# A quarter of the gathered second rows summed on TensorE instead of VectorE, with sixteen gelu slots and twelve first products ahead

## Chip, cores and metric

One core of one Trainium2 chip. The metric is device time in microseconds (us), of which the median of several runs is quoted. The kernel before takes 1690.52 us, median of three runs (1689.63 to 1690.55).

## What is computed

One DeepNorm layer over 512 tokens of width 1024. The first half (attention with forget gates, a convolution branch, gates, an output projection, a layer norm) is not touched. The second half is a product-key expert retrieval: for every token the 128 best of 16384 experts (8 heads of 16) are found, each with a gate.

```python
ue = jnp.take(u_tab, ei, axis=0)
a = jnp.einsum('thkd,td->thk', ue, xi)
wgt = (jax.nn.gelu(a.astype(jnp.float32)) * gi).astype(xi.dtype)
ve = jnp.take(v_tab, ei, axis=0)
return jnp.einsum('thk,thkd->td', wgt, ve)
```

The result is scaled by a gate row, added to the layer's input and layer-normalised. All is float32.

## The kernel before, in words

**Two ways to the retrieval.** For 384 tokens (three tiles of 128, `TD = 3`) the kernel is dense: the expert table is cut into 128 chunks of 128 experts, and each chunk has a *first product* (u-chunk times tokens, 24 matmuls of 128x384), a gelu on ScalarE, a multiplication by the gates, and a *second product* (two halves of the v-chunk, each 9 matmuls of 128x512, since every product is made of a high and a low part in three matmuls, `three`, lines 1725 to 1729). For the last 128 tokens, the *own* tile, it is sparse: GpSimd gathers for every slot j of 128 (`SLOTS`) one row of the table per token, 128 rows of 4 KB. VectorE turns a gathered u-row into a dot product (`dot`, line 1384), and later adds a gathered v-row times its weight into `acc[:, TD, :]` (`own_row`, line 1616). The gathers land in a ring of eight slots; gather j waits until the slot's last user is done (lines 675 and 714).

**Stages.** The first 80 chunks (`SPILL`) have only their first product, beside the search for the experts; their gelu goes to memory (`gelu_ahead`) and comes back later as `gback`. Then `FILL = 8` further first products are made ahead (chunks 80 to 87, until `PRE = 88`), while the last gates are written to memory (`gates_by_key`). SyncE then loads the gates back (`gring`, line 547), the first v-chunks (`vraw`, line 522) and the rest of the u-chunks.

**Groups.** After that come 16 groups of 8 chunks (`GR = 8`). Group g has a first half of eight steps k (in each, while there are any left, one first product and the first half of second product k) and a second half of eight steps (the other half of second product k). Groups 0 to 4 make the first products of chunks 88 to 127; groups 5 to 15 have only second products. In each step VectorE makes the low part of a v-chunk (`low_v`, line 1584), in the first half of groups 0 to 4 also that of a u-chunk (`low_u`, line 1379), and in the second half the gated gelu of the next group (`weigh`, line 1572, and `low_w`, line 1578, between which ScalarE makes the high part, line 944). The instructions stand in a hand-written order on each engine. v-chunks have four converted slots (`VR`), and their raw rows four, eight from group 6 on.

**Quotas.** The dots are spread by `DOT_F` over the FILL steps and by `DOT_G` over the first-half steps of groups 0 to 4 (24 a group). The own rows are spread by `ROWS_OF` and `rows_at` evenly over all 16 steps of groups 4 to 14: 6, then 13 in each of eight groups, then 12 and 6. `gelz` has eight slots; the gelu of chunk c in the groups waits for `weigh` of chunk c - 88 (line 897 onwards). At the start of group 12 (`ROW_GROUP`) SyncE loads the layer's input `xfin` and two broadcast rows (lines 593 to 596, together 3 MB), ahead of that group's v-chunks. In the last group `own_sum` (line 1633) finishes the own tile in steps 4 and 5.

A matmul of 32 columns into a quarter of a bank's partitions stands already in the kernel at `mod_rows` (line 1816); sixteen of them run one behind the other.

Of the kernel before, what the change touches and what calls it, by code (L numbers as in the profile page):

```python
# [13 lines left out]
P = 128  # L14
# [81 lines left out]
ROWS_OF = (6,) + (13,) * 8 + (12, 6)  # L96
assert sum(ROWS_OF) == SLOTS

# [4 lines left out]
FILL = 8  # L103
# [3 lines left out]
PS = 8  # L107
VR = 4
# [3 lines left out]
DOT_F = (0, 0, 0, 1, 1, 2, 2, 2)  # L112
DOT_G = (3, 3, 3, 3, 3, 3, 3, 3)
# [12 lines left out]
W_GROUP = BESIDE - 2  # L126
V_GROUP = W_GROUP + 1
ROW_GROUP = NG - 4
assert len(DOT_F) == FILL and len(DOT_G) == GR
assert sum(DOT_F) + sum(DOT_G) * V_GROUP == SLOTS  # L130
# [3 lines left out]
def build(nc, x, cb, ccol, w_modn, b_modc, w_modt, wblk, b_fc, conv_wc, conv_vec, keys_t, u_t, u_tab, v_tab, rows, out):  # L134
    with ExitStack() as ctx:
# [50 lines left out]
        gelz = sb("gelz", [P, PS, TN], F32, 88)  # L186
        x2s = sb("x2s", [P, D], F32, 100)
# [19 lines left out]

        gback = sb("gback", [P, 3, 2, TN], F32, 4)
        xfin = sb("xfin", [P, TT, D], F32, 32)
# [30 lines left out]
        idxN = small("idxN", [P, SLOTS], I32)  # L240
        own_g = small("own_g", [P, SLOTS], F32)
# [118 lines left out]
        own_w = sem("own_w")  # L360
        own_v = sem("own_v")
        u_in = [sem(f"u_in{i}") for i in range(RAW)]
# [37 lines left out]
        def v_row(i):  # L400
# [6 lines left out]
            return row, v_in[slot], 16 * (uses + 1), before  # L407

# [59 lines left out]
        def _(sp):  # L468
# [89 lines left out]
            load_u(PRE)  # L558
# [6 lines left out]
            for c in range(PRE + 1, PRE + RAW):  # L565
                load_u(c)
# [23 lines left out]
            for g in range(NG):  # L590
                if g == ROW_GROUP:
                    sp.wait_ge(x1_out, 16)
                    sp.dma_start(xfin[:, 0:TD, :], x1_dram[1:TT].rearrange("t p d -> p t d")).then_inc(x1_in, 16)
# [3 lines left out]
                first_half(g)  # L597
# [16 lines left out]
        def _(pool):  # L614
# [94 lines left out]
            for j in range(SLOTS):  # L709
                if j < RING:  # L710
                    pool.wait_ge(dot_r, SLOTS - RING + j + 1)
                else:
# [3 lines left out]
                    in_offset=bass.IndirectOffsetOnAxis(ap=idxN[:, j:j + 1], axis=0)).then_inc(ring_in[j % RING], 16)  # L716

# [7 lines left out]
        def _(act):  # L725
# [167 lines left out]
            def gelu(c):  # L893
                m = c // 4
                act.wait_ge(u_mm, c + 1)
                if c >= PRE:
                    act.wait_ge(w_mul, c - PRE + 1)
                elif c % 4 == 0 and m > 1:
                    act.wait_ge(gel_out[m % 2], 16 * (m // 2))
                nc.scalar.activation(gelz[:, c % PS, :], bank[c % 2][:, 0:TN], ACT.Gelu_apprx_tanh).then_inc(gel_r, 1)  # L900
# [69 lines left out]
            def group(g, last=False):  # L970
                for k in range(GR):
# [3 lines left out]
                    if k and c < CH:  # L975
# [6 lines left out]
                if PRE + GR * g < CH:  # L982
                    gelu(PRE + GR * g + GR - 1)
                if g == W_GROUP:
                    act.wait_ge(dot_r, SLOTS)
                    nc.scalar.activation(own_a[:], own_a[:], ACT.Gelu_apprx_tanh).then_inc(own_gel, 1)
# [22 lines left out]
        def _(dve):  # L1009
# [407 lines left out]
            def select(s):  # L1417
# [97 lines left out]
                if s in numbers:  # L1515
                    link(last)
                    last = nc.vector.tensor_copy(numbers[s][:].rearrange("p (h k) -> p h k", k=TOPK), sel[:, 0, :, :])
                last.then_inc(sel_r, 1)
                beside(15)

            def transposed(s):

                dve.wait_ge(selT_mm, s)
                nc.vector.tensor_copy(selT[:, 2, :], bank[2][:, P:2 * P])
# [34 lines left out]
            def weigh(g, k):  # L1559
# [3 lines left out]
                if g < BESIDE:  # L1563
                    dve.wait_ge(gel_r, c + 1)
                    src = gelz[:, c % PS, :]
# [39 lines left out]
            own_next = iter(range(SLOTS))  # L1605

            def own_row():

                j = next(own_next)
                dve.wait_ge(ring_in[j % RING], 16 * ((SLOTS + j) // RING + 1))  # L1610
                if j == 0:
                    dve.wait_ge(own_w, 1)
                    nc.vector.tensor_scalar(acc[:, TD, :], ring[:, 0, :], own_a[:, 0:1], None, ALU.mult).then_inc(own_v, 1)
                else:
                    dve.wait_ge(own_v, j)
# [511 lines left out]
```

## Time and profile before

| quantity | value |
|---|---|
| median of three runs | 1690.52 us |
| the profiled execution | 1690.79 us, span 1689.0 us |
| TensorE, VectorE, ScalarE, GpSimd busy | 1566.8, 1388.3, 687.6, 678.0 us |
| chain that ended last | TensorE 60%, VectorE 25%, issue 5%, DMA 5%, ScalarE 3% |
| moved by DMA | 422.22 MB, 250 GB/s over the span |

The busy time of TensorE counts matmuls that overlap, so its share says little of how far it is from its limit; what matters is where it sits idle and who ends that. A row of the timeline reads: start in us, duration in us, engine, line, operation, output and input, how many are merged, and in brackets how long the engine had been idle and who ended that. "vlo L1584" is the low part of a v-chunk. A row of a stretch reads: its length, then the busy time of TensorE, its weight loads, VectorE, ScalarE and GpSimd with their instructions, the granted TensorE clock as a share of 2.4 GHz, the busy share of the DMA engines and the GB/s moved.

### The profile page before, as it was taken

Reading aid. Unit: us, or ns where it says so; the run is one execution under the profiler, and the core shown is the slowest. Engines: PE = TensorE matmul, PEld = TensorE weight load, DVE = VectorE, ACT = ScalarE, POOL = GpSimd, SP = SyncE. Lnnn points to the kernel's source line nnn. Section 1 sums busy time; section 2 is a strip of 40 time slices with the busy share of each in tenths; the row PEclk is TensorE's granted clock in tenths of the full one; section 3 lists DMA queues with packets and bytes.
Section 4 is the critical chain, followed back from the end, with each engine's and each line's share of the span. In section 5 each row is a group of like instructions: output and inputs, shape, how many; then the busy total and the mean of one; then the engine's idle time right before and its main releaser. Section 6 shows DMA issues by size and latency. Waiting matters only on the chain.

```text
span 1689.0 us, 22167 instructions
## 1 busy us (share of the span) xinstructions
PE 1566.8 (93%) x7772; PEld 1361.4 (81%) x7772; DVE 1388.3 (82%) x2725; ACT 687.6 (41%) x1037; POOL 678.0 (40%) x450
## 2 busy tenths in 40 slices
PE   5999999994999999999998999999988999998986
PEld 3887777773899999999997998988967777776775
DVE  5489776888489799979966987977978888887888
ACT  4335565424334345545553343343333333333342
POOL 0210000002035778677763844746643443333301
PEclk9999999997999999999999999999999999999999
DMA  8323234462676657667789989989899999999962
GB/s 350 100 76 125 88 100 162 149 205 83 229 253 206 176 159 185 180 192 183 205 229 351 395 325 339 374 310 367 285 338 366 357 382 378 362 385 384 364 223 81
DMA packets 180894, 422.22 MB, mean 250 GB/s; under 512 B 33584, under 2 KB 66480, under 8 KB 180528
## 3 DMA queue, kind: packets, MB, share of 16 engines
q1 hardware_dynamic: 90688, 264.44, 43.8%
q0 software_dynamic: 57200, 139.58, 24.9%
q10 hardware_dynamic: 32896, 16.78, 3.6%
q8 instruction: 63, 1.03, 0.2%
q14 instruction: 47, 0.39, 0.1%
HBM read 375.55 MB, written 45.15 MB: 249 GB/s over the span
## 4 chain that ended last, share of the span: by engine, by line
PE 60%; DVE 25%; issue 5%; DMA 5%; ACT 3%; SPq 0%; DVEq 0%; POOL 0%; ACTq 0%; POOLq 0%
PE bank L1727 18%; PE bank L1728 18%; PE bank L1729 18%; DVE vlo L1584 2%; DVE el L1578 2%; DVE wf L1572 2%; DVE one L1544 2%; DMA gring<-gates_by_key 2%; DVE wlo L1379 2%; DVE one L1542 2%; ACT eh L944 2%; DVE one L1546 2%; DMA gates_by_key<-stage 1%; PE bank L1873 1%; PE bank L2008 1%
## 5 line engine op out<-in xcount | busy, mean ns | idle before, releaser
L1727 PE MATMUL bank<-act_hi,whi 128*128 128x384 f32 (+1 forms) x1352 | 482.2, 357 | 12.7 <-ACT gelz L900 4.5
L1729 PE MATMUL bank<-act_hi,wlo 128*128 128x384 f32 (+1 forms) x1352 | 473.1, 350 | 0.0
L1728 PE MATMUL bank<-act_lo,whi 128*128 128x384 f32 (+1 forms) x1352 | 473.0, 350 | 0.0
L1727 PE MATMUL bank<-vhi,eh 128*128 128x512 f32 x768 | 306.7, 399 | 46.3 <-DVE vlo L1584 46.3
L1728 PE MATMUL bank<-vlo,eh 128*128 128x512 f32 x768 | 302.7, 394 | 0.0
L1729 PE MATMUL bank<-vhi,el 128*128 128x512 f32 x768 | 302.5, 394 | 0.0
L1727 PEld LDWEIGHTS bank<-act_hi,whi 128*128 128x128 f32 x1352 | 256.1, 189 | 30.9 <-issue 7.9
L1728 PEld LDWEIGHTS bank<-act_lo,whi 128*128 128x128 f32 x1352 | 256.0, 189 | 13.9
L1729 PEld LDWEIGHTS bank<-act_hi,wlo 128*128 128x128 f32 x1352 | 255.5, 189 | 13.4
L691 POOL DMA_INDIRECT gates_by_key<-selW,selS x128 | 233.6, 1825 | 70.0 <-issue 47.5
L675 POOL DMA_INDIRECT ring<-in_u_tab_dram,idxN x128 | 200.5, 1567 | 149.5 <-DVE ring L1384 98.0
L714 POOL DMA_INDIRECT ring<-in_v_tab_dram,idxN x128 | 151.2, 1182 | 231.6 <-DVE acc L1616 221.6
L1727 PEld LDWEIGHTS bank<-vhi,eh 128*128 128x128 f32 x768 | 145.9, 190 | 89.7 <-DVE vlo L1584 60.7
L953 ACT ACTIVATE vhi<-vraw 128x512 fp32r<-128x512 f32 x256 | 155.8, 623 | 138.6 <-PE bank L1729 130.3
L1584 DVE TENSOR_TENSOR vlo<-vraw,vhi 128x512 fp32r<-128x512 f32 x256 | 176.3, 696 | 36.2 <-ACT vhi L953 33.7
L1379 DVE TENSOR_TENSOR wlo<-raw,whi 128x1024 fp32r<-128x1024 f32 x108 | 131.9, 1222 | 59.1 <-ACT whi L891 57.2
L1729 PEld LDWEIGHTS bank<-vhi,el 128*128 128x128 f32 x768 | 146.0, 190 | 31.4
L1728 PEld LDWEIGHTS bank<-vlo,eh 128*128 128x128 f32 x768 | 146.1, 190 | 29.0 <-issue 0.5
L900 ACT ACTIVATE gelz<-bank 128x384 f32<-128x384 f32 x128 | 63.3, 494 | 260.2 <-PE bank L1729 247.1
L1616 DVE SCALAR_TENSOR_TENSOR acc<-ring,own_a,acc 128x1024 f32<-128x1024 f32 x127 | 162.6, 1280 | 0.0
L944 ACT ACTIVATE eh<-wf 128x384 fp32r<-128x384 f32 x128 | 67.2, 525 | 231.9 <-DVE wf L1572 229.4
L1384 DVE SCALAR_TENSOR_TENSOR ring<-ring,x2s 128x1024 f32<-128x1024 f32 x128 | 150.7, 1221 | 7.9 <-DMA ring<-in_u_tab_dram,idxN 6.6
(237 smaller groups left out, 1978.4 us busy)
## 6 DMA issues: line engine op xcount, KB each, us to landing
raw<-in_u_t_dram SPq DMA_DIRECT2D x128, 512.0 KB
vraw<-in_v_tab_dram SPq DMA_DIRECT2D x256, 256.0 KB
raw<-in_wblk_dram SPq DMA_DIRECT2D x61, 512.0 KB, 4.2
gring<-gates_by_key SPq DMA_DIRECT2D x32, 768.0 KB
raw<-in_w_modt_dram SPq DMA_DIRECT2D x32, 512.0 KB, 3.4
gates_by_key<-stage ACTq DMA_DIRECT2D x8, 2048.0 KB
gelu_ahead<-gelz SPq DMA_DIRECT2D x20, 768.0 KB
gback<-gelu_ahead SPq DMA_DIRECT2D x40, 384.0 KB
```

The lines of the kernel that those rows point to most:

```text
L675: pool.indirect_dma_start(out=ring[:, j % RING, :], out_offset=None, in_=u_tab, in_offset=bass.IndirectOffsetOnAxis(ap=idxN[:, j:j + 1], a ...
L691: pool.indirect_dma_start(out=gates_flat, out_offset=bass.IndirectOffsetOnAxis(ap=selS[:, n:n + 1], axis=0), in_=selW[:, n:n + 1], in_offs ...
L714: pool.indirect_dma_start(out=ring[:, j % RING, :], out_offset=None, in_=v_tab, in_offset=bass.IndirectOffsetOnAxis(ap=idxN[:, j:j + 1], a ...
L944: nc.scalar.activation(eh[:, k, :], wf[:, k % 2, :], ACT.Copy).then_inc(w_hi, 1)
L953: nc.scalar.activation(hi_slot, row, ACT.Copy).then_inc(v_hi, 1)
L1379: nc.vector.tensor_tensor(wlo[:, c % SPL, :], raw[:, c % RAW, :], whi[:, c % SPL, :].bitcast(F32), ALU.subtract).then_inc(u_lo, 1)
L1384: nc.vector.scalar_tensor_tensor(out=ring[:, j % RING, :], in0=ring[:, j % RING, :], scalar=1.0, in1=x2s[:], op0=ALU.mult, op1=ALU.mult, a ...
L1584: nc.vector.tensor_tensor(lo_slot, v_row(2 * GR * g + n)[0], hi_slot.bitcast(F32), ALU.subtract).then_inc(v_lo, 1)
L1616: nc.vector.scalar_tensor_tensor(out=acc[:, TD, :], in0=ring[:, j % RING, :], scalar=own_a[:, j:j + 1], in1=acc[:, TD, :], op0=ALU.mult, o ...
L1727: mm(o, wh, mh, start=start, stop=False)
L1728: mm(o, wh, ml, start=False, stop=False)
L1729: return mm(o, wl, mh, start=False, stop=stop)
```

## The change

Of the 128 v-rows of each own token, 96 (`OWN`) are still summed by VectorE. The other 32 (`QSLOTS`) go to TensorE in eight *quads*. One gather brings the 32 rows of four tokens into the 128 partitions; a quad is four such gathers (`qring`, 2 MB) and eight matmuls of 32 columns by 512, with weights that are zero but for the token's own column (`wz`). They accumulate in banks 0 and 1, which `own_sum` adds. One quad is made in each of groups 5 to 12, after step 10 of the group. The indices and weights are laid out for this once (`shared_out`, `transposed`, `eye`, one transpose in FILL, one in group 4). The quad's gathers stand on the GpSimd queue among the own gathers. FILL is 12 (`PRE = 92`), so that group 4 has four first products and not eight; `gelz` has sixteen slots. `DOT_G` has 27 dots a group in groups 0 to 3 and 8 in group 4. The own rows are 3 in group 4 and 9 or 10 in each of groups 5 to 14, six of them in the first half's first six steps. `xfin` is loaded after the first half of group 13 and waits for the last quad.

```diff
-FILL = 8
+SHARED = 4
+QSLOTS = P // SHARED
+OWN = SLOTS - QSLOTS
+QUADS = P // (4 * SHARED)
+IN_STRIP = QUAD // SHARED
+FILL = 12
+GS = 16
-DOT_F = (0, 0, 0, 1, 1, 2, 2, 2)
-DOT_G = (3, 3, 3, 3, 3, 3, 3, 3)
+DOT_F = (0, 0, 0, 1, 1, 1, 1, 1, 1, 2, 2, 2)
+DOT_G = (4, 3, 3, 4, 3, 3, 4, 3)
+DOT_W = (2, 2, 2, 2, 0, 0, 0, 0)
+OWN_AT = [(0, 0, 0, 0, 0, 0, 0, 0, 0, 0, 1, 0, 1, 0, 1, 0)] + [(1, 1, 1, 1, 1, 1, 0, 0, 0, 1, 0, 1, 0, 1, n, 0) for n in
+                                                                (1, 0, 0, 1, 0, 0, 1, 0, 0, 0)]
+QUAD_STEP = GR + 2
-W_GROUP = BESIDE - 2
+W_GROUP = (CH - PRE) // GR
-ROW_GROUP = NG - 4
+ROW_GROUP = NG - 3
...
+    _rows = sum(sum(n) for n in OWN_AT[:_i]) + sum(OWN_AT[_i][:QUAD_STEP]) + RING if _i else RING // 2
+    QUAD_ROWS[_rows] = _i
...
-            for c in range(PRE):
+            for c in range(PRE - 1):
                 load_u(c)
...
             for g in range(NG):
+                first_half(g)
                 if g == ROW_GROUP:
                     sp.wait_ge(x1_out, 16)
+                    sp.wait_ge(quad_mm, QUADS)
...
+            def quad_rows(i):
+                if i == 0:
+                    pool.wait_ge(selT_sb, TT - 1)
+                    pool.wait_ge(u_lo, low_before(CH)[0])
+                else:
+                    pool.wait_ge(quad_mm, i)
+                for j in range(4):
+                    four = j * IN_STRIP + i
+                    pool.indirect_dma_start(
+                        out=qring[:, j, :], out_offset=None, in_=v_tab,
+                        in_offset=bass.IndirectOffsetOnAxis(ap=idxT[:, four:four + 1], axis=0)).then_inc(quad_in, 16)
...
+            for j in range(OWN):
+                if j in QUAD_ROWS:
+                    quad_rows(QUAD_ROWS[j])
+                own_gather(j)
...
-                if c >= PRE:
-                    act.wait_ge(w_mul, c - PRE + 1)
+                if c >= SPILL + GS:
+                    act.wait_ge(w_mul, c - SPILL - GS + 1)
...
-                dve.wait_ge(own_v, SLOTS)
+                dve.wait_ge(own_v, OWN)
+                link(nc.vector.tensor_tensor(acc[:, TD, cut], acc[:, TD, cut], bank[half][:, :], ALU.add))
...
+                    if g == W_GROUP and k == 4:
+                        dve.wait_ge(wT_mm, 1)
+                        link(shared_out(wT, bank[0]))
+                        for j in range(4):
+                            part = slice(j * IN_STRIP, (j + 1) * IN_STRIP)
+                            nc.vector.tensor_tensor(wz[:, part, :],
+                                                    wT[:, part].unsqueeze(2).broadcast_to([P, IN_STRIP, QUAD]),
+                                                    eye[:], ALU.mult).then_inc(wz_r, 1)
...
+            def quad(i):
+                if i == 0:
+                    pe.wait_ge(wz_r, 4)
+                    pe.wait_ge(g_row, 2)
+                pe.wait_ge(quad_in, 64 * (i + 1))
+                for half in range(2):
+                    for j in range(4):
+                        last = mm(bank[half][j * QUAD:(j + 1) * QUAD, :], wz[:, j * IN_STRIP + i, :],
+                                  qring[:, j, half * HALF:(half + 1) * HALF], start=i == 0, stop=i == QUADS - 1)
+                last.then_inc(quad_mm, 1)
...
+                        if GR + k == QUAD_STEP and 0 <= g - V_GROUP < QUADS:
+                            quad(g - V_GROUP)
```

## Rows read from the trace of the kernel before

**Rows 1.** The page's costliest groups: busy, mean ns, idle before, releaser.
```profile
L1727 PE MATMUL bank<-vhi,eh 128*128 128x512 f32 x768 | 306.7, 399 | 46.3 <-DVE vlo L1584 46.3
...
L1616 DVE SCALAR_TENSOR_TENSOR acc<-ring,own_a,acc 128x1024 f32<-128x1024 f32 x127 | 162.6, 1280 | 0.0
...
L1384 DVE SCALAR_TENSOR_TENSOR ring<-ring,x2s 128x1024 f32<-128x1024 f32 x128 | 150.7, 1221 | 7.9 <-DMA ring<-in_u_tab_dram,idxN 6.6
```

**Rows 2.** TensorE's timeline: its wait before step 3, groups 8, 9, 11, 12, 14.
```profile
1379.18 0.50 PE L1727 MATMUL bank<-vhi,eh 128*128 128x512 f32 x1 [2.05 <-DVE vlo L1584]
...
1417.02 0.50 PE L1727 MATMUL bank<-vhi,eh 128*128 128x512 f32 x1 [2.05 <-DVE vlo L1584]
...
1494.29 0.50 PE L1727 MATMUL bank<-vhi,eh 128*128 128x512 f32 x1 [2.05 <-DVE vlo L1584]
...
1538.69 0.51 PE L1727 MATMUL bank<-vhi,eh 128*128 128x512 f32 x1 [1.81 <-DVE vlo L1584]
...
1614.31 0.50 PE L1727 MATMUL bank<-vhi,eh 128*128 128x512 f32 x1 [2.07 <-DVE vlo L1584]
```

**Rows 3.** TensorE's timeline: two second-product triples, one behind the other.
```profile
1655.28 0.39 PE L1727 MATMUL bank<-vhi,eh 128*128 128x512 f32 x1
1655.96 0.39 PE L1727 MATMUL bank<-vhi,eh 128*128 128x512 f32 x1
```

**Rows 4.** VectorE's timeline, one step in the second half of group 9.
```profile
1443.28 1.28 DVE L1616 SCALAR_TENSOR_TENSOR acc<-ring,own_a,acc 128x1024 f32<-128x1024 f32 x1
1444.47 0.69 DVE L1584 TENSOR_TENSOR vlo<-vraw,vhi 128x512 fp32r<-128x512 f32 x1
1445.08 0.55 DVE L1572 TENSOR_TENSOR wf<-gback,gring 128x384 f32<-128x384 f32 x1
1446.22 0.56 DVE L1578 TENSOR_TENSOR el<-wf,eh 128x384 fp32r<-128x384 f32 x1 [0.59 <-ACT eh L944]
1446.69 1.28 DVE L1616 SCALAR_TENSOR_TENSOR acc<-ring,own_a,acc 128x1024 f32<-128x1024 f32 x1
```

**Rows 5.** DMA by stretch (1371 to 1409, 1500 to 1530, 1388 to 1403 us).
```profile
DMA packets 5067, 14.27 MB, mean 375 GB/s; under 512 B 563, under 2 KB 563, under 8 KB 5065
...
DMA packets 3769, 11.99 MB, mean 400 GB/s; under 512 B 390, under 2 KB 390, under 8 KB 3767
...
DMA packets 1993, 6.10 MB, mean 407 GB/s; under 512 B 217, under 2 KB 217, under 8 KB 1993
```

**Rows 6.** Line 900 in 1000 to 1066 us (first and last start), and busy times there.
```profile
L900 ACT ACTIVATE gelz<-bank x9: 472/492/493, 999.6 to 1066.1; 128x384 f32<-128x384 f32 x9
...
1000.00:1066.00 66.00, 66.00 (x336) 60.14 (x335) 56.04 (x90) 24.49 (x40) 38.58 (x25) 1.00 0.92 345
```

**Rows 7.** Timelines of ScalarE, SyncE and TensorE around the end of FILL.
```profile
896.50 0.49 ACT L900 ACTIVATE gelz<-bank 128x384 f32<-128x384 f32 x1 [2.72 <-PE bank L1729]
...
893.66 0.33 SPq L547 DMA_DIRECT2D gring<-gates_by_key  x1
...
909.30 0.41 PE L1727 MATMUL bank<-act_hi,whi 128*128 128x384 f32 x1 [4.51 <-ACT gelz L900]
...
927.41 0.69 PE L1727 MATMUL bank<-act_hi,whi 128*128 128x384 f32 x1 [3.75 <-DVE wlo L1379]
```

**Rows 8.** TensorE's timeline: its waits where group 5 begins.
```profile
1251.49 0.50 PE L1727 MATMUL bank<-vhi,eh 128*128 128x512 f32 x1 [0.75 <-DVE vlo L1584]
1254.90 0.50 PE L1727 MATMUL bank<-vhi,eh 128*128 128x512 f32 x1 [1.08 <-DVE vlo L1584]
...
1260.32 2.72 PE L1933 MATMUL bank<-dg,consts 128*128 128x512 f32 x4 [3.08 <-DVE dg L1243]
```

**Rows 9.** TensorE's timeline: the 32-column matmuls of `mod_rows`.
```profile
35.89 1.92 PE L1816 MATMUL bank<-modn,cwide 128*32 128x512 f32 x16
```

**Rows 10.** The last group: `own_sum` on VectorE, and TensorE's wait behind it.
```profile
1648.65 0.68 DVE L1633 TENSOR_TENSOR acc<-acc,rows 128x512 f32<-128x512 f32 x1
...
1662.34 0.50 PE L1727 MATMUL bank<-vhi,eh 128*128 128x512 f32 x1 [2.82 <-DVE vlo L1584]
```

More of the change, by code:

```diff
@@ L125 @@
 ZEROS = 16
-W_GROUP = BESIDE - 2
+W_GROUP = (CH - PRE) // GR
 V_GROUP = W_GROUP + 1
-ROW_GROUP = NG - 4
+ROW_GROUP = NG - 3
 assert len(DOT_F) == FILL and len(DOT_G) == GR
-assert sum(DOT_F) + sum(DOT_G) * V_GROUP == SLOTS
+assert sum(DOT_F) + sum(DOT_G) * W_GROUP + sum(DOT_W) == SLOTS
+assert sum(sum(n) for n in OWN_AT) == OWN and V_GROUP + QUADS <= ROW_GROUP
+QUAD_ROWS = {}
+for _i in range(QUADS):
+    _rows = sum(sum(n) for n in OWN_AT[:_i]) + sum(OWN_AT[_i][:QUAD_STEP]) + RING if _i else RING // 2
+    QUAD_ROWS[_rows] = _i
+assert len(QUAD_ROWS) == QUADS
 assert [sum(n) for n in LOWS] == [STEPS[0], STEPS[2]]
@@ L240, in build @@
         idxN = small("idxN", [P, SLOTS], I32)
+        idxT = small("idxT", [P, QSLOTS], I32)
         own_g = small("own_g", [P, SLOTS], F32)
@@ L564, in _ @@
                 load_v(0, k, 0)
-            for c in range(PRE + 1, PRE + RAW):
+            for c in range(PRE - 1, PRE + RAW):
                 load_u(c)
@@ L1603, in last_sum @@
                 return bn(xfin, t, half)
[L1605 to L1615, printed above, removed]
-                    nc.vector.scalar_tensor_tensor(out=acc[:, TD, :], in0=ring[:, j % RING, :],
-                                                   scalar=own_a[:, j:j + 1], in1=acc[:, TD, :],
-                                                   op0=ALU.mult, op1=ALU.add).then_inc(own_v, 1)
@@ L1620, in rows_at, with own_rows @@
[L1620 to L1627 removed]
+            own_next = iter(range(OWN))
+            def own_rows(g, step):
+                at = g - W_GROUP
+                for _ in range(OWN_AT[at][step] if 0 <= at < len(OWN_AT) else 0):
+                    j = next(own_next)
+                    dve.wait_ge(ring_in[j % RING], 16 * ((SLOTS + j) // RING + 1))
+                    if j == 0:
+                        dve.wait_ge(own_w, 1)
+                        nc.vector.tensor_scalar(acc[:, TD, :], ring[:, 0, :], own_a[:, 0:1], None,
+                                                ALU.mult).then_inc(own_v, 1)
+                    else:
+                        dve.wait_ge(own_v, j)
+                        nc.vector.scalar_tensor_tensor(out=acc[:, TD, :], in0=ring[:, j % RING, :],
+                                                       scalar=own_a[:, j:j + 1], in1=acc[:, TD, :],
+                                                       op0=ALU.mult, op1=ALU.add).then_inc(own_v, 1)
@@ L1992, in sel_T @@
                 need(pe, gt_sb, NBT * (s - TT + LAID))
-                for r in range(2):
+                for i, r in enumerate((0, 1) if ORDER[s] else (1,)):
                     src = sel[:, r, :, :].rearrange("p h k -> p (h k)")
-                    last = nc.tensor.transpose(bank[2][:, r * P:(r + 1) * P], src, ident[:])
+                    last = nc.tensor.transpose(bank[2][:, i * P:(i + 1) * P], src, ident[:])
                 last.then_inc(selT_mm, 1)
```

96 lines of the change are left out of this document (64 added, 32 removed).

## The prediction, made before the changed kernel was built or run

> **What bounds the kernel now.** I read the page, then TensorE's waits one by one over the last 800 us, then what VectorE did ahead of them, then the DMA of those stretches. Second products wait 46.3 us in all for the low part of a v-chunk, while VectorE never idles ahead of an own row and 7.9 us ahead of a dot [rows 1]. So gathered rows are there in time, and VectorE is late with something else. The waits stand at the same place in each group: the one before step 3 comes 37.84 us apart in undisturbed groups (1379.18 to 1417.02), 38.6 on average over the next two, and 44.4 once (1494.29 to 1538.69), in the group in which `xfin` is loaded [rows 2]. TensorE alone would need 16 x 9 matmuls; three take 1655.96 - 1655.28 = 0.68 us [rows 3], so 16 x 3 x 0.68 = 32.6 us. The missing 5.2 us are VectorE's. A step of its second half goes row 1.19, low v 0.61, weigh 1.14 (with 0.59 waiting for ScalarE), low w 0.47: 3.41 us from row to row [rows 4], against 2.04 of TensorE. A group costs VectorE 16 x 0.61 + 8 x 1.61 + 13 x 1.20 = 9.8 + 12.9 + 15.6 = 38.3 us, near the 37.84 seen. Groups 5 to 14 are VectorE's.
>
> Close behind stands DMA. A group moves 14.27 MB at 375 GB/s [rows 5]; by the code it is 16 x 256 + 2 x 768 + 4 x 384 + 13 x 512 KB = 14.16 MB. With the `xfin` load queued it moved 400 GB/s for 30 us, and then the group took 44.4 us [rows 2, 5]: loads came late there. So about 400 GB/s is what this mixture reaches when there is always work queued, and today's 375 is not far below.
>
> Groups 0 to 4 are TensorE's: it is busy for 66.00 of 66 us [rows 6], and a group takes 66.5 us (eight intervals between gelus, 999.6 to 1066.1). Ahead of them it waits 4.51 us (the gates' store must land before SyncE may issue `gring` at 893.66, and no product is left to make) and 3.75 us [rows 7].
>
> **The sum, against the profiled execution's 1690.79 us** (0.3 above the median of 1690.52, which I neglect).
>
> *FILL of 12.* A first product is worth (66.5 - 32.6) / 8 = 4.2 us. The product of chunk 87 ended at 909.30 - 4.51 = 904.8; the gelu at 999.6 is that of chunk 98. Between them lie 11 first products and 18 half second products, 46.2 + 36.7 = 83 us, in 94.8 us: 11.8 us were lost, of which 8.3 are the two waits and the rest a slower start (the matmul after the second wait takes 0.69 us, not 0.41, as at the lower level, 1.2 GHz) [rows 6, 7]. Four more products keep TensorE busy until about 904.8 + 4 x 4.2 = 921.6 us, while what must be ready (gates, v, first `weigh`) is started no later than now: SyncE's extra u-loads 89 and 90 depend on low parts made before 893.7. I leave 1 us of waiting for VectorE's serial weigh and low steps. Gain 10.8. The moved products are taken out of group 4, one for one. The extra transposes, four small copies and one broadcast copy lie beside first products, where VectorE has gaps: nothing.
>
> *Groups 0 to 3.* Three more dots are 3 x 1.22 = 3.7 us [rows 1]; VectorE is busy 56.0 of 66 us, plus 4.7 of waits for ScalarE in weigh [rows 4, 6], so about 5 are free. DMA: 1.57 MB more on 345 GB/s x 66 us = 22.8 MB makes 24.3 MB, 61 us at 400 GB/s. Both fit, closely. I charge 1 us, bounds 0 and 6 (1.5 a group if the v-loads, four slots deep, come late).
>
> *Entering group 5.* TensorE waits 0.75 + 1.08 + 3.08 = 4.9 us there, behind own rows and the diagonals [rows 8]. Three own rows fewer in the second half (-3.6), the masks and weights in (twelve small operations, four of them in the first half, no row for their shapes; between 0.15 and 0.7 each, I take 0.25 as for small tiles, +2.0 in the second half): gain 1.6, bounds -3 and +4.
>
> *A quad on TensorE.* Sixteen 32-column matmuls take 1.92 us [rows 9], so the eight of a quad take 0.96 us; with the change of shape 1.1. Bounds 0.96 and, if the four column strips did not overlap, 8 x 0.8 = 6.4. The row has the same shape and strips: 1.1. A quad group is 32.6 + 1.1 = 33.7 us of TensorE.
>
> *Groups 5 to 12.* VectorE does 9.3 rows, not 13: 37.84 - 3.7 x 1.20 = 33.4 us, and six of them lie in the first half, where it now has to wait for slots, so the halves fit. Both engines allow about 34. DMA: 9.3 + 4 gathers, not 13, so 14.27 + 0.17 = 14.44 MB. In 34 us that is 425 GB/s, above the 400 of [rows 5]. At 400 it is 36.1 us. So DMA takes over as the bound: I take 36.1, bounds 34.0 and 38.5 (today's 375 GB/s). Which load comes late I expect to be v (SyncE) or `quad_in`: GpSimd holds its own gathers back until TensorE has finished a quad, and VectorE's rows wait behind them, with eight rows in the ring for the nine or so steps until they are back.
>
> About this the Trainium skill has two figures. "DMA: Bandwidth & Descriptors", section "Where 436 GB/s comes from", says that between HBM and SBUF the HBM side binds a core at about 358 GB/s. "HBM Reference" says that a core that streams alone reaches about 425. The first would make a quad group 40 us and leave nothing of this part's gain, the second 34. This trace moved 375 over whole groups, so it contradicts the first; it never held 425 over a group.
>
> *Group 13 with `xfin`.* The group with this load takes 44.4 - 37.84 = 6.6 us more now. It moves to a group without a quad and behind that group's first gates; I charge 3 (bounds 0 and 7). Group 13: 32.6 + 1 + 3 = 36.6.
>
> *From step 3 of group 5 to step 3 of group 14.* Now 1614.31 - 1262.4 (1260.32 plus the gate row's 2.1) = 351.9 us [rows 2, 8]. After: 8 x 36.1 + 36.6 = 325.4. Gain 26.5. Group 14 was TensorE's already (six rows only) and stays at 33 with nine.
>
> *Tail.* Two additions from PSUM, 2 x 0.7 us with their links, ahead of the low v-parts for which TensorE waits 2.82 us [rows 10]: loss 1.4.
>
> Sum: 10.8 - 1 + 1.6 + 26.5 - 1.4 = 36.5 us; 1690.8 - 36.5 = **1654 us**.
>
> **Rivals.**
>
> *TensorE is the bound.* DMA yields what is asked. Quad groups 34.0 (-17), `xfin` 1 (-2), groups 0 to 3 free (-1): 1634 us. For it: no DVE row waits for its gather today, and 15 us of an ordinary group ran at 407 [rows 5]. Against it: 425 GB/s would have to hold for 270 us. The 425 of the HBM page gives the same time. Chance 0.27.
>
> *DMA stays at 375 GB/s.* Quad groups 38.5 (+19), group 13 and groups 0 to 3 +3: 1676 us. For it: the v-rows are 2 KB pieces by the code, and the 407 is from 15 us that the faster kernel would need on average. Chance 0.20. By the page's 358 it would be 8 x 3.9 = 31 us more than my forecast, 1685.
>
> *The quads' bursts starve SyncE's loads: slower.* Four gathers of 512 KB are issued at once, with up to eight others in flight. The one 3 MB burst in the trace cost 6.6 us. If each 2 MB burst cost as much on top of 36.1, it would be 8 x 6.6 = 53 us: 1707 us. It decides from 36.5 / 8 = 4.6 us a quad. Against it: gathers on GpSimd's queue are half of the bytes already, and the total hardly changes; `xfin` stood in front of the v-loads on their own queue, and quads do not. Chance 0.05.
>
> **Numbers.** My forecast 0.45, the three rivals 0.27, 0.20, 0.05, and 0.03 for something else. The range 1631 to 1677 takes in the first rival with 3 us of room and about half of the second; outside lie about 0.18. A difference of 0.2% (3.4 us) is what a measurement of this kernel can tell from none. Faster by more: all of the forecast and of the first two rivals, 0.93. Slower by more: 0.05. Within: 0.02.
>
> **What would show it.** FILL: no wait for a gelu near 905 us, the first second product near 922. Groups 5 to 12: the distance of equal steps 36 (mine), 34 (first rival) or 38.5 (second); TensorE's waits now behind a v-load or a quad's gathers and not behind own rows; DMA at 400 GB/s. Quad: eight matmuls in about 1 us. Own rows with idle time ahead of them would show the ring too short. Wrong I would be if VectorE still ended most of TensorE's waits, or groups 0 to 3 grew beyond 68 us.

## The result, and the profile after

The changed kernel takes 1676.8 us (median of four, 1672.68 to 1677.81), the kernel before 1690.5 beside it: a ratio of 0.9914 [0.9897, 0.9931]. A second set of four runs gave 1675.3 us and 0.9916 [0.9887, 0.9945]. That is 14 us of gain where 36.5 were forecast. The profiled execution is the fastest of its four, 1672.68 us; its span is 18.1 us under that of before. I therefore read a profile of the second set beside it (span 1676.2, "the second profile"). One of the six runs of a later kernel, two_moves, took 5121.83 us in the slow state and stands in no median here.

The page of the changed kernel, its costliest groups:

```profile
span 1670.9 us, 22384 instructions
...
PE 1575.6 (94%) x7902; PEld 1359.4 (81%) x7902; DVE 1357.4 (81%) x2713; ACT 688.9 (41%) x1037; POOL 668.0 (40%) x450
...
PE 48%; DVE 27%; DMA 9%; POOL 6%; issue 5%; ACT 4%; SPq 0%; DVEq 0%; ACTq 0%
...
L1807 PE MATMUL bank<-vhi,eh 128*128 128x512 f32 x768 | 305.2, 397 | 22.7 <-DVE vlo L1652 22.6
```

Second products now wait 22.6 us for low v parts, not 46.3 [rows 1]: half of VectorE's lateness is gone. TensorE's timeline, at its larger waits (step 3 of group 13 at 1552.20, of group 14 at 1593.30 and of group 15 at 1628.41), answers to [rows 2, 7, 8, 10]:

```profile
938.74 0.69 PE L1807 MATMUL bank<-act_hi,whi 128*128 128x384 f32 x1 [4.59 <-DVE wlo L1432]
...
1258.41 1.96 PE L2013 MATMUL bank<-dg,consts 128*128 128x512 f32 x4 [2.53 <-DVE dg L1296]
...
1276.64 1.92 PE L2136 MATMUL bank<-qring,wz 128*32 128x512 f32 x16
...
1317.78 1.92 PE L2136 MATMUL bank<-qring,wz 128*32 128x512 f32 x16
...
1531.58 1.92 PE L2136 MATMUL bank<-qring,wz 128*32 128x512 f32 x16
...
1552.20 0.50 PE L1807 MATMUL bank<-vhi,eh 128*128 128x512 f32 x1 [1.55 <-DVE vlo L1652]
...
1566.26 0.50 PE L1807 MATMUL bank<-vhi,eh 128*128 128x512 f32 x1 [3.57 <-DVE vlo L1652]
...
1593.30 0.50 PE L1807 MATMUL bank<-vhi,eh 128*128 128x512 f32 x1 [1.55 <-DVE vlo L1652]
...
1628.41 0.50 PE L1807 MATMUL bank<-vhi,eh 128*128 128x512 f32 x1 [1.66 <-DVE vlo L1652]
...
1644.26 0.50 PE L1807 MATMUL bank<-vhi,eh 128*128 128x512 f32 x1 [2.17 <-DVE vlo L1652]
```

Three stretches, each from a point that both kernels have to the next. The gate row (lines 2013 and 1933) is the four matmuls that stand before step 3 of group 5:

| stretch | before, us | after, us | second profile, us | gained in the first / second profile (forecast) |
|---|---|---|---|---|
| start to the gate row | 1260.32 | 1258.41 | 1265.00 | 1.9 / -4.7 (11.4) |
| gate row to step 3 of group 14 | 354.0 | 334.9 | 333.6 | 19.1 / 20.4 (26.5) |
| from there to the last wait | 48.0 | 51.0 | 51.0 | -3.0 (-1.4) |

So the largest part of the shortfall is ahead of the first quad. There the wait for a gelu at 909 is gone, as forecast, but the second one stayed, 4.59 us instead of 3.75, and small ones follow in groups 1 to 3 where there were none. ScalarE's timeline shows the last gelu of the first half of groups 0 to 3, first in the changed kernel's profile, then in the second:

```profile
976.49 0.49 ACT L953 ACTIVATE gelz<-bank 128x384 f32<-128x384 f32 x1 [3.49 <-PE bank L1809]
...
1043.04 0.49 ACT L953 ACTIVATE gelz<-bank 128x384 f32<-128x384 f32 x1 [3.49 <-PE bank L1809]
...
1110.23 0.49 ACT L953 ACTIVATE gelz<-bank 128x384 f32<-128x384 f32 x1 [3.49 <-PE bank L1809]
...
1177.79 0.49 ACT L953 ACTIVATE gelz<-bank 128x384 f32<-128x384 f32 x1 [3.49 <-PE bank L1809]
```

```profile
976.86 0.49 ACT L953 ACTIVATE gelz<-bank 128x384 f32<-128x384 f32 x1 [3.49 <-PE bank L1809]
...
1044.27 0.49 ACT L953 ACTIVATE gelz<-bank 128x384 f32<-128x384 f32 x1 [3.49 <-PE bank L1809]
...
1113.62 0.49 ACT L953 ACTIVATE gelz<-bank 128x384 f32<-128x384 f32 x1 [3.49 <-PE bank L1809]
...
1184.85 0.49 ACT L953 ACTIVATE gelz<-bank 128x384 f32<-128x384 f32 x1 [3.49 <-PE bank L1809]
```

The periods are 66.5, 67.2 and 67.6 us in the one, 67.4, 69.3 and 71.2 in the other; before they were 66.5 [rows 6]. In the groups with quads the distances from quad to quad are 41.1, 35.0, 35.0, 36.2, 36.0, 35.4 and 36.2 us, against 37.84 before and 36.1 forecast.

### The profile page after: what moved, and what is told of

Its sections match the earlier page's. It is cut to its first block, busy times and chain, and to the rows that moved or that the text cites. A ratio compares the mean times of both kernels' runs of the same rounds, so it can differ in the third digit from the quotient of the medians.

```text
span 1670.9 us, 22384 instructions
## 1 busy us (share of the span) xinstructions
PE 1575.6 (94%) x7902; PEld 1359.4 (81%) x7902; DVE 1357.4 (81%) x2713; ACT 688.9 (41%) x1037; POOL 668.0 (40%) x450
## 4 chain that ended last, share of the span: by engine, by line
PE 48%; DVE 27%; DMA 9%; POOL 6%; issue 5%; ACT 4%; SPq 0%; DVEq 0%; ACTq 0%
PE bank L1807 14%; PE bank L1808 14%; PE bank L1809 14%; DMA vraw<-in_v_tab_dram 7%; POOL ring L708 6%; DVE wlo L1432 3%; DVE vlo L1652 3%; DVE wf L1640 2%; DVE one L1612 2%; DVE one L1610 2%; ACT eh L997 2%; DMA ring<-in_u_tab_dram,idxN 2%; DVE one L1614 2%; DVE el L1646 2%; DVE ring L1437 2%
## 5 line engine op out<-in xcount | busy, mean ns | idle before, releaser
L1807 PE MATMUL bank<-vhi,eh 128*128 128x512 f32 x768 | 305.2, 397 | 22.7 <-DVE vlo L1652 22.6
L708 POOL DMA_INDIRECT ring<-in_u_tab_dram,idxN x128 | 185.0, 1445 | 131.7 <-DVE ring L1437 78.5
L760 POOL DMA_INDIRECT ring<-in_v_tab_dram,idxN x96 | 116.5, 1213 | 237.8 <-DVE acc L1687 203.7
L997 ACT ACTIVATE eh<-wf 128x384 fp32r<-128x384 f32 x128 | 67.2, 525 | 219.1 <-DVE wf L1640 219.1
L942 ACT ACTIVATE whi<-raw 128x1024 fp32r<-128x1024 f32 x128 | 134.6, 1053 | 14.2 <-DMA raw<-in_u_t_dram 14.1
```

Source lines behind the costliest of these rows:

```text
L708: pool.indirect_dma_start(out=ring[:, j % RING, :], out_offset=None, in_=u_tab, in_offset=bass.IndirectOffsetOnAxis(ap=idxN[:, j:j + 1], a ...
L760: pool.indirect_dma_start(out=ring[:, j % RING, :], out_offset=None, in_=v_tab, in_offset=bass.IndirectOffsetOnAxis(ap=idxN[:, j:j + 1], a ...
L942: nc.scalar.activation(whi[:, c % SPL, :], raw[:, c % RAW, :], ACT.Copy).then_inc(u_hi, 1)
L997: nc.scalar.activation(eh[:, k, :], wf[:, k % 2, :], ACT.Copy).then_inc(w_hi, 1)
L1807: mm(o, wh, mh, start=start, stop=False)
```

## Experiments

Fifteen runs were made, of fourteen kernels and of the changed kernel once more, in four sets, each set beside the kernel before. A set's differences to the changed kernel are given through the ratios to before (0.9914 to 0.9916 for the changed kernel); 0.001 of ratio is 1.7 us. The intervals reach 2.5 to 5 us to either side, so a difference of 2 or 3 us between two kernels is not told from none by the times alone.

### What bounds groups 5 to 12?

```diff
-                for j in range(4):
+                for j in range(4 if i == 0 else 0):
...
-                pe.wait_ge(quad_in, 64 * (i + 1))
+                pe.wait_ge(quad_in, 64)
```

> The changed kernel, but only the first quad's four rows sets are gathered; the other seven quads multiply the same rows again, so 28 gathers of 512 KB (14.7 MB) are left out and the own tile's result is not the reference's. Every matmul and every wait for TensorE stays. Theory A (groups 5 to 12 are bound by DMA at about 400 GB/s): the distance from quad to quad falls from 35.0 to 36.2 us to TensorE's own 34.6 to 35.0 (32.6 plus 1.92 for the quad), group 5 to 6 from 41.1 to under 37, the v-loads' waits vanish, and the kernel is 8 to 14 us faster than the changed one (1663 to 1669 us). Theory B (TensorE and VectorE are the bound there and the gathers ride beside them): the same time within 3 us, 1674 to 1680.

1672.5 us, ratio 0.9903 [0.9874, 0.9932]: about 2 us better by the ratios, not 8 to 14, and not clear of the intervals. DMA from quad to quad, in the changed kernel (1353 to 1388 us, groups 7 to 8) and with the gathers left out:

```profile
DMA packets 5008, 14.08 MB, mean 401 GB/s; under 512 B 553, under 2 KB 553, under 8 KB 5004
```

```profile
DMA packets 4471, 12.10 MB, mean 345 GB/s; under 512 B 497, under 2 KB 497, under 8 KB 4467
```

and TensorE's quads in the second kernel:

```profile
1353.04 1.92 PE L2136 MATMUL bank<-qring,wz 128*32 128x512 f32 x16
...
1388.06 1.92 PE L2136 MATMUL bank<-qring,wz 128*32 128x512 f32 x16
...
1424.21 1.92 PE L2136 MATMUL bank<-qring,wz 128*32 128x512 f32 x16
```

Two megabytes a group fewer, and the distances are 35.0 and 36.15 as they were (35.0 and 36.2). TensorE is busy throughout a 35.0: 16 x 3 x 0.68 = 32.6, a quad 1.92, and half a microsecond of small gaps. The 36.2 stand where a group has ten own rows: TensorE waits 1.09 us for VectorE there with the gathers and without. Only in some places do transfers cost time: 41.1 from the first quad to the second became 36.65, and of the later distances 36.0 and 35.4 became 35.0 and 35.05. From the first quad to the last it is 254.9 us in the first profile and 252.1 in the second, against 249.0 without the gathers. ScalarE's waits for raw v rows fell from 67.0 to 19.6 us in all, almost all of which had been covered.

VectorE stands at 35 us as well. Group 14 has nine own rows and no quad, and so has group 13; in xfin14 (below) group 13 has no load of `xfin` either. TensorE's step 3 of groups 13 and 14 in xfin14:

```profile
1558.05 0.50 PE L1807 MATMUL bank<-vhi,eh 128*128 128x512 f32 x1 [1.52 <-DVE vlo L1652]
...
1593.06 0.50 PE L1807 MATMUL bank<-vhi,eh 128*128 128x512 f32 x1 [1.52 <-DVE vlo L1652]
```

That is 35.01 us for a group without a quad, and in the changed kernel group 14 takes 1628.41 - 1593.30 = 35.11, each time with a wait for VectorE's low part at its end. DMA was slack in the latter, at 194 GB/s. In the kernel before, group 14 with six own rows took 32.8, from 1614.31 [rows 2] to step 3 of group 15:

```profile
1647.12 0.39 PE L1727 MATMUL bank<-vhi,eh 128*128 128x512 f32 x1
```

So with nine rows VectorE alone holds a group at 35, and on TensorE the quad fills time in which it would otherwise wait. No run left out the quads' matmuls, so this is read from groups without a quad and not tried on groups with one.

### Each half of the change alone

The filling alone: the kernel before with `FILL = 12`, sixteen gelu slots, the new dots and the change's order of SyncE's u-loads, no quads.

```diff
-FILL = 8
+FILL = 12
...
+GS = 16
...
-DOT_F = (0, 0, 0, 1, 1, 2, 2, 2)
-DOT_G = (3, 3, 3, 3, 3, 3, 3, 3)
+DOT_F = (0, 0, 0, 1, 1, 1, 1, 1, 1, 2, 2, 2)
+DOT_G = (4, 3, 3, 4, 3, 3, 4, 3)
+DOT_W = (2, 2, 2, 2, 0, 0, 0, 0)
```

> The kernel before with only the first part of the change: FILL of 12, sixteen gelu slots, 27 dots a group in groups 0 to 3 and 8 in group 4; all 128 own rows on VectorE at the old places. The prediction's sum gives 10.8 - 1 = about 10 us of gain (1681). What the changed kernel's profile shows (the wait at 905 us gone, but one of 4.6 us at 939 and groups of 67.2 and 67.6 us) gives 2 to 4 us (1687 to 1689). If it is 10, the loss in the changed kernel comes from the quads' additions to this stretch; if 3, from this part by itself.

1692.4 us, 1.0016 [0.9999, 1.0032]: nothing gained. In its trace the wait at 909 is gone, the next is 4.58 us, groups 1 to 3 have waits of 1.25 to 2.1 us, and the gate row is at 1261.38, a microsecond later than before. At the end of group 0's first half (gelu at 975.93, four products of 4.15 us more made than at 964.52 before) it was still 5.2 us ahead.

The quads alone, in two forms. Both undo the filling in the changed kernel (`FILL = 8`, 24 dots a group also in group 4, masks and weights of the quads a few steps later):

```diff
-FILL = 12
+FILL = 8
...
-DOT_G = (4, 3, 3, 4, 3, 3, 4, 3)
-DOT_W = (2, 2, 2, 2, 0, 0, 0, 0)
+DOT_G = (3, 3, 3, 3, 3, 3, 3, 3)
+DOT_W = (3, 3, 3, 3, 3, 3, 3, 3)
```

> The changed kernel with its quads, its gathers and its row placement, but with eight first products ahead and 24 dots a group as before; what makes the quads' weights stands a few steps later. It is the other half of the change, where the twelve ahead alone gave 1692 against 1689. Theory A (twelve ahead is worth nothing, since VectorE is full from 938 to 1215 either way; the whole gain is the quads', 15 to 19 us by the group distances): 1673 to 1679, the gate row at 1258 to 1263. Theory B (twelve ahead is worth its 4 to 10 us once the quads' relief follows): 1680 to 1688, with the gate row 4 to 8 us later than in the changed kernel.

1682.5 us, 0.9951 [0.9937, 0.9966]. By the letter that was theory B, but the trace shows a wait that neither kernel has, at the filling:

```profile
906.42 0.69 PE L1807 MATMUL bank<-act_hi,whi 128*128 128x384 f32 x1 [6.00 <-DVE wlo L1432]
```

The change had also moved two of SyncE's u-loads behind the gates, and with only eight products ahead the last of them needs its u-chunk at once. The second form gives the loads back their order:

```diff
-            for c in range(PRE - 1):
+            for c in range(PRE):
                 load_u(c)
...
+            load_u(PRE)
...
-            for c in range(PRE - 1, PRE + RAW):
+            for c in range(PRE + 1, PRE + RAW):
```

> The same with SyncE's loads in the order of the kernel before (the ninth column of the first table is sent for ahead of the gates, not behind them). Theory A (twelve ahead is worth nothing or nearly so; the late column made the wait of 6.0 us at 906 and the gate row at 1267.3): the waits at filling are again 4.5 and 3.8 us, the gate row is at 1259 to 1263 and the time is 1674 to 1678, that of the changed kernel. Theory B (twelve ahead is worth 4 to 7 us): 1680 to 1683 again.

1676.0 us, 0.9911 [0.9888, 0.9935]: the time of the whole change. Its waits, at the filling and at the gate row (of which this is the first record):

```profile
907.94 0.66 PE L1808 MATMUL bank<-act_hi,whi 128*128 128x384 f32 x1 [4.17 <-ACT gelz L954]
...
926.05 0.69 PE L1808 MATMUL bank<-act_hi,whi 128*128 128x384 f32 x1 [4.03 <-DVE wlo L1433]
...
1261.54 1.19 PE L2014 MATMUL bank<-dg,consts 128*128 128x512 f32 x1 [0.69 <-DVE dg L1297]
```

With both waits back it reaches the gate row within the 1258.4 to 1265.0 of the changed kernel. Twelve products ahead, as the change has them, are worth nothing that these intervals of 4 us can tell; the 14 us come with the quads. This kernel also keeps the change's placement of the own rows, which alone does nothing in the kernel before (rows_first_half, below), and its load of `xfin` one group later, which was not tried alone.

### Why the filling's gain does not arrive

> The changed kernel with the serial chain of group 0 (weigh, copy to exact, low part of the second rows) spread over the last four of the twelve chunks ahead, instead of standing whole behind the last of them. Theory A (the forecast's term at the filling fell short because this chain was still in the way, as TensorE's 4.6 us wait at 938.5 for a low part that VectorE had not yet made shows): that wait falls under 1 us, the gate row is multiplied 3 to 6 us sooner than in the changed kernel (1258.4 and 1265.0 in its two profiles), and the time is 4 to 7 us below its 1676. Theory B (VectorE has no spare time in groups 0 to 4, so what is won at 938 is waited away before group 5): the wait goes too, but the waits of groups 1 to 3 grow by as much and the time stays within 2 us of 1676.

```diff
             for j in range(FILL):
-                if j == FILL - 2:
+                if j == FILL - 4:
...
-            low_v(0, 1)
-            weigh(0, 2)
-            low_w(0, 2)
+                if j == FILL - 3:
+                    low_v(0, 1)
+                    weigh(0, 2)
+                    low_w(0, 2)
```

1677.9 us, 0.9932 [0.9907, 0.9957]: no gain. SyncE's load of the second gates also stands earlier in it, ahead of the first v-loads. The wait at 938 fell to 0.86 us, but waits for a gelu of 0.90 and 2.10 came at 918 and 924, so that 3.9 us of waiting are left of 4.6 there, and one of 2.28 for a low v part came at 984. At the end of group 0's first half it was 2.7 us ahead of the changed kernel (973.8), at the end of group 1's 1.4 behind its first profile (1044.4) and level with its second (1044.3).

> The changed kernel with 24 of VectorE's dot products in each of groups 0 to 4, as before, instead of 27 and 8 later ones; what is no longer done there stands in the chunks of the steps before group 5. Theory A (27 dots fill VectorE over, so that groups 1 to 3 last 67.2 to 71.2 us instead of 66.5): group periods return to 66.5 to 67, TensorE's waits in these groups to under 1 us each, and the time is 3 to 8 us below 1676. Theory B (VectorE's total up to the gate row is what counts, wherever the dots stand): the periods shrink but the steps between group 4 and the gate row grow by the same, and the time stays within 2 us of 1676.

```diff
-DOT_G = (4, 3, 3, 4, 3, 3, 4, 3)
-DOT_W = (2, 2, 2, 2, 0, 0, 0, 0)
+DOT_G = (3, 3, 3, 3, 3, 3, 3, 3)
+DOT_W = (4, 4, 4, 4, 4, 0, 0, 0)
```

1680.0 us, 0.9943 [0.9922, 0.9964]: 4 to 5 us slower than the changed kernel, which neither theory has. The periods are 66.5 us again, without a wait, and yet the gate row comes at 1264.94. For group 4 has only four first products to hide twenty dots, and VectorE, with its low v parts queued behind them, waits for the dots' gathers; then TensorE waits. From its timelines (VectorE, TensorE):

```profile
1231.86 1.23 DVE L1437 SCALAR_TENSOR_TENSOR ring<-ring,x2s 128x1024 f32<-128x1024 f32 x1 [2.38 <-DMA ring<-in_u_tab_dram,idxN]
```

```profile
1233.76 0.79 PE L1807 MATMUL bank<-vhi,eh 128*128 128x512 f32 x1 [5.42 <-DVE vlo L1652]
```

> The changed kernel with 116 of VectorE's 128 dot products made over 256 of the 1024 columns, the other columns left out; gathers and everything else as they are, which takes some 90 us of VectorE's work out of 890 to 1225. Theory A (a full VectorE is what makes groups 0 to 3 longer than 66.5 us and brings the waits behind them): periods of 66.3 to 66.6, TensorE's waits in groups 1 to 3 gone, the gate row at 1250 to 1257, time 4 to 9 us below 1676. Theory B (the gathers of the dots' rows or their landing set it): VectorE waits for the ring's gathers instead, the gate row stays at 1258 to 1265 and the time within 2 us of 1676.

```diff
-                nc.vector.scalar_tensor_tensor(out=ring[:, j % RING, :], in0=ring[:, j % RING, :], scalar=1.0,
-                                               in1=x2s[:], op0=ALU.mult, op1=ALU.mult,
+                cols = D // 4 if j >= 12 else D
+                nc.vector.scalar_tensor_tensor(out=ring[:, j % RING, 0:cols], in0=ring[:, j % RING, 0:cols], scalar=1.0,
+                                               in1=x2s[:, 0:cols], op0=ALU.mult, op1=ALU.mult,
```

1670.0 us, 0.9880 [0.9851, 0.9909]: 6 us better. Busy times from 1078.90 to 1146.80 us (TensorE, its loads, VectorE, ScalarE, GpSimd, clock, DMA), first the changed kernel, then this one:

```profile
1078.90:1146.80 67.90, 67.09 (x339) 60.70 (x338) 58.78 (x95) 24.71 (x40) 40.56 (x28) 1.00 0.93 353
```

```profile
1078.90:1146.80 67.90, 67.90 (x344) 61.70 (x343) 39.55 (x98) 25.99 (x41) 28.73 (x29) 1.00 0.94 368
```

DMA moves even more, and TensorE is never idle; the gate row comes at 1255.03. The periods are 66.5, 66.4 and 66.5. So it is VectorE's work, not the gathers' bytes, that made groups 1 to 3 longer. Here the lead at the end of group 0's first half, 4.3 us (gelu at 976.80), is not lost on the way: at the gate row it is 5.3.

VectorE was not full by its busy share, 58.8 of 67.9 us; it was behind TensorE step by step. Its low v parts around the end of group 2's first half, in the changed kernel:

```profile
1105.74 0.69 DVE L1652 TENSOR_TENSOR vlo<-vraw,vhi 128x512 fp32r<-128x512 f32 x1
...
1113.21 0.69 DVE L1652 TENSOR_TENSOR vlo<-vraw,vhi 128x512 fp32r<-128x512 f32 x1
...
1118.39 1.36 DVE L1652 TENSOR_TENSOR vlo<-vraw,vhi 128x512 fp32r<-128x512 f32 x2
...
1121.37 0.69 DVE L1652 TENSOR_TENSOR vlo<-vraw,vhi 128x512 fp32r<-128x512 f32 x1
...
1123.64 0.69 DVE L1652 TENSOR_TENSOR vlo<-vraw,vhi 128x512 fp32r<-128x512 f32 x1
```

A step with low u, low v and four dots takes it 7.5 us (0.6 of it waiting for a gather), one with three dots 5.2, and TensorE's step in that half 6.27. In the second half, without dots, a step takes VectorE 2.27 us (0.59 of it waiting for ScalarE) and TensorE 3 x 0.68 = 2.04. It catches up only in the steps with three dots.

> The changed kernel with 26 dots a group and twelve in group 4, and nothing else. Theory A (27 dots overfill VectorE in groups 1 to 3, 24 leave twenty for group 4 where their gathers come too late; 26 and 12 avoid both): periods of groups 1 to 3 at 66.5 to 67.2, the gate row at 1255 to 1259, 1671 to 1674. Theory B (the 3.7 us by which the two moves with 26 dots beat those with 27 were spread of the runs): 1675 to 1677.

```diff
-DOT_G = (4, 3, 3, 4, 3, 3, 4, 3)
-DOT_W = (2, 2, 2, 2, 0, 0, 0, 0)
+DOT_G = (4, 3, 3, 3, 3, 3, 4, 3)
+DOT_W = (3, 3, 3, 3, 0, 0, 0, 0)
```

1673.2 us, 0.9894 [0.987, 0.9918]: 2 to 4 us better, in the direction of theory A, though the intervals overlap. Its profile does not bear theory A out: the periods are 67.2, 67.8 and 66.5 us and the gate row is at 1259.46.

### Group 5 and the last rows' load

> The changed kernel with the 2.4 MB of the last input rows (the load of xfin) one group later, beside group 14 instead of 13. Theory A (it holds up the second rows' loads: ScalarE waits 9.6 us for a raw row there and TensorE 3.6 to 4.6 us near 1570): these waits shrink to under 2 us and the time is 3 to 5 us below 1676. Theory B (the load only moves, and the wait moves with it into group 14 or to the end, where the rows are needed): time within 2 us of 1676, with a wait of 3 us or more after 1600. If the rows come too late for the last sums, it is slower by up to 5.

```diff
-ROW_GROUP = NG - 3
+ROW_GROUP = NG - 2
```

1673.0 us, 0.9898 [0.9875, 0.9921]: 3 us better by the ratios, with intervals that overlap. The trace shows more: the wait of 3.57 us at 1566 is gone, one of 1.40 stands at 1605, group 13 takes 35.0 us instead of 41.1 and group 14, now with the load, 36.8 instead of 35.1.

> The changed kernel with eight raw slots for the second rows already in group 5 instead of from group 6, by waiting for the first weights' release one group sooner. Theory A (from the first quad to the second it is 37.0 to 41.1 us instead of 35 to 36, because only four loads of v are under way there): the distance falls to 35 to 37 and the time is 2 to 5 us below 1676. Theory B (TensorE's own 34.6 and VectorE's row work set it, and the loads only follow): no change, within 2 us of 1676.

```diff
-        DEEP_FROM = 2 * GR * BESIDE
+        DEEP_FROM = 2 * GR * (BESIDE - 1)
...
-                    sp.wait_ge(w_mul, GR * BESIDE)
+                    sp.wait_ge(w_mul, GR * (BESIDE - 1))
```

1673.4 us, 0.9910 [0.9887, 0.9933]. The mechanism is there, but alone its gain in the whole time can't be told from nothing: from the first quad to the second it is now 36.15 us, not 37.0 to 41.1 (the first records of the two):

```profile
1280.66 0.64 PE L2136 MATMUL bank<-qring,wz 128*32 128x512 f32 x4
...
1316.81 0.64 PE L2136 MATMUL bank<-qring,wz 128*32 128x512 f32 x4
```

> The kernel before with the 13 own rows of groups 5 to 12 at other steps: nine in the first half and four in the second (before: six or seven in each), nothing else. If VectorE's total in a group is the bound (38 us), nothing changes: 1690 +- 3. If TensorE's waits came only from the crowded second half, it gains up to 8 x 4 = 32 us, and the redistribution and not the quads would be what pays in the change.

```diff
-                return (step + 1) * n // (2 * GR) - step * n // (2 * GR)
+                if n != 13:
+                    return (step + 1) * n // (2 * GR) - step * n // (2 * GR)
+                return (1, 1, 1, 1, 1, 1, 1, 1, 1, 0, 1, 1, 0, 1, 1, 0)[step]
```

The kernel before with `rows_at` placing 9 of the 13 rows in the first half: 1691.7 us, 1.0011 [0.9995, 1.0027]. Placement alone does nothing while VectorE has 38.3 us of work in the group: the groups take 38.3 us, and TensorE's waits only stand elsewhere.

### Put together

> The changed kernel with both moves that seemed to help: the last input rows' load beside group 14, and eight raw slots for the second rows already in group 5. Theory A (each takes out a wait of its own, about 3 and 2 us): 1669 to 1672, first to second quad under 37 us, no wait over 2.2 us after 1500. Theory B (one wait covers the other, or the differences were the chip's own spread): 1673 to 1677.

1668.1 us, 0.9879 [0.9853, 0.9905]: the edits of xfin14 and deep5 together. It fits theory A, a little below its time, at 36.2 us from the first quad to the second and with no wait over 2.15 us after 1500.

> The two moves, and 26 dots a group with twelve in group 4, between the changed kernel's 27 and 8 and the 24 and 20 that made VectorE wait for gathers in group 4. Theory A (each arrangement has a cost of its own, 27 in groups 1 to 3 and 20 in group 4, and the middle has the least of both): 1 to 3 us below the two moves alone. Theory B (VectorE's sum up to the gate row is all that counts): within 1 us of it.

1665.3 us (1663.31 to 1668.1), 0.9855 [0.9832, 0.9877]. This is a version that beats both kernels: 24.5 us under before by the ratio, 10 under the changed one. Its edits are the two moves and that of dots26; the 26 dots took 4 us off, more than expected, with intervals that overlap; its gate row is at 1257.13, against 1261.28 with the two moves alone. Its quads are 36.1, 35.1, 35.0, 37.2, 35.9, 35.1 and 38.0 us apart.

> The two moves and 26 dots, with the serial chain of group 0 spread over the last four chunks ahead. Theory A (the chain's 4.6 us wait is real time once VectorE has room behind it): 1660 to 1664, with the waits of groups 0 to 3 under 1 us each. Theory B (VectorE's sum from 913 to the gate row is the bound there, and a wait taken out at 938 comes back as low parts that are late): within 2 us of the 1665.3 without it.

1664.2 us, 0.9841 [0.9816, 0.9866]: the wait of 4.60 at 938 is gone here too; two of 2.16 and 2.10 us for a gelu came at 919 and 925, and one of 2.63 at 1249. Again no gain that can be told. But the waits at the filling are 4.3 us in all instead of 4.6, and the last gelu of group 0's first half comes at 975.54 with this edit and 975.53 without: here the wait was only moved ahead, and whether a lead would have lasted was not tried.

> The changed kernel once more, unchanged, as the measure for the others on this chip: 1676.8 +- 3 us, in all theories.

It gave the second profile used above: the same code reached the gate row 6.6 us later than in the first profile and lost less afterwards. VectorE waited 10.9 us for the dots' gathers in it, against 5.9.

## Why the prediction was wrong, by its steps

**FILL of 12 (10.8 us forecast) is the step that failed.** The wait at 909 did go. But at the end of group 0's first half TensorE was only 16.6 - 12.0 = 4.6 us ahead (four products of 4.15 us more had been made, and the gelu came at 976.5 instead of 964.5), and at the gate row 1.9 ahead or 4.7 behind. The 10.8 counted as gained not only that wait but the second one and the slow start behind it. I had allowed 1 us for VectorE's serial chain, where it cost 4.59; the chain of weigh, ScalarE's copy and low w for eight chunks runs from 917.99 to 935.95, the low u part that TensorE needs stands behind it (937.46), and TensorE restarts on a 0.69 us matmul at a granted clock of 0.50, the lower of its two levels, as it did before [rows 7]. The deeper error is that a wait taken from TensorE was booked as time taken from the end. With VectorE behind TensorE in groups 0 to 3, the lead is lost: fill12_alone was 5.2 us ahead and reached the gate row 1.1 behind, early_chain's 2.7 us were gone a group later, and with eight products ahead the time is the same. With VectorE's dots cut down (narrow_dots) the lead arrives. two_moves26_early shows nothing on this, since it was never ahead of two_moves26.

**Groups 0 to 3 (1 us forecast).** They cost 1.8 us in the first profile and 8.5 in the second (the three periods against 66.5), beyond the bound of 6. I had set 56.0 busy and 4.7 waiting microseconds against 66, found 5 free and put 3.7 of dots into them. Over a whole group that sum still fits; step by step it doesn't, neither where four dots stand (7.5 us against 6.27) nor in the second half (2.27 against 2.04). The dots' gathers add to it: VectorE waited 10.9 us for them in the second profile and 5.9 in the first. narrow_dots gives 6 us back, and shows that neither the gathers' bytes nor the v-loads are needed to explain it.

**Entering group 5 (1.6 forecast).** The waits are 0.43 + 1.08 + 2.53 = 4.0 us instead of 4.9: 0.9 gained, within the bounds. From the last gelu of group 3's first half to the gate row, four first products allowed for, TensorE nevertheless took 0.8 us longer than before; the transposes for the quads stand there, and waits under 0.4 us that I did not follow.

**A quad on TensorE (1.1 us).** It takes 1.92 us, for eight matmuls. The row I went by [rows 9] says x16, and I took that for sixteen matmuls. But the records of the quads' line in the changed kernel are 128, for the 64 matmuls of eight quads, two for each; and `mod_rows` issues eight in one call, too:

```profile
L2136 PE MATMUL bank<-qring,wz x128: 592/592/617, 1276.6 to 1532.9; 128*32 128x512 f32 x128
```

So a quad group is 35.0 us of TensorE, not 33.7. What the first rival was priced at (34.0 a quad group) could not have come. The eight on four column strips take 0.24 us each; the 0.8 us of my upper bound is in no row.

**Groups 5 to 12 at 36.1 us.** They took 291.7 us from step 3 of group 5 to step 3 of group 13 (1260.5 to 1552.2), forecast 288.8. The size was right and the reason wrong. DMA did move 391 and 393 GB/s from the first quad to the third and 398 to 402 in the five distances after them, as the forecast asked, and the rows would have passed as its proof; yet with 345 to 350 GB/s the distances from the second quad on are the same within about 1 us. The limits happen to lie together: 14.08 MB at 401 GB/s are 35.1 us, TensorE with a quad 35.0, and VectorE with nine rows 35.0. That last one I had at 33.4 (37.84 - 3.7 x 1.20), so by these groups a cheaper quad would have brought little either. On this trace the 358 GB/s of the Trainium skill ("DMA: Bandwidth & Descriptors", "Where 436 GB/s comes from") was passed in all of these groups.

**Group 13 with `xfin` (36.6 forecast).** It took 1593.30 - 1552.20 = 41.1 us. Without the load the same group takes 35.0 in xfin14, not the 33.6 that I had, so the load cost 6.1 and not 3, within its bound of 7, and the rest is VectorE's mis-sized part again. Behind the 3 MB ScalarE awaited a v row for 9.6 us, and TensorE a low part for 3.57. A group later the load costs 36.8 - 35.1 = 1.7.

**Tail (-1.4 forecast).** -3.0. Group 14, which I had left as it was, takes 35.1 us with nine rows instead of 32.8 with six, and ends in a wait of 1.66: 2.3 us that were not in the sum. From step 3 of group 15 to the last wait it is 0.6 longer, where the two additions were priced at 1.4.

Together: 9.5 us short up to the gate row, 2.9 in groups 5 to 12, 4.5 in group 13, 1.6 in the tail make 18.5; the profiled execution is indeed 18.4 us above the forecast for it. The median lies 4 us higher still; the second profile shows where such an execution loses them, in groups 0 to 4. Of the rivals none came as described. DMA at 375 GB/s named the time, 1676, but the rate was 398 to 402 in most groups. That 1676.8 still lies inside the range of 1631 to 1677 is luck: the range reached that far for this rival, and it did not come.

## What to carry to other kernels

A wait removed ahead of a stretch is worth only what the feeder of that stretch can keep up with: compare its work with the time step by step, with its own waits in it, and not over a whole group. When work moves from one engine to another, look also for groups that lack the moved work: if they take as long, the engine it was taken from is still a limit. When a resource runs at the rate that was called its limit, that is no proof that it binds; take away some of its load and see if the time follows. Before a duration is divided by a count, look up in the code how many instructions the count stands for.

## What was not expected of the hardware

The DMA engines moved 401 GB/s over a group of 35.0 us in which TensorE waited for nothing, and 402 over the next of 36.2, with 4 KB and 2 KB rows and gathers mixed; before, the most seen over such a time was 400 for 30 us [rows 5]. A plain matmul of 32 columns by 512 is recorded twice, and eight of them on four column strips take 1.92 us, 0.24 each, in a place where one 128-column matmul of the same 512 takes 0.23. And the same code differs by 6.6 us in when it reaches the gate row, while whole executions differ by 5 us: in the later one VectorE waited 5 us more for the dots' gathers, and what decides when those land was not tried.
